# The gather of an expert's tokens, multiplied the other way round

## The reference

```python
def moe_ffn(h, router, w_gate, w_up, w_down):
    xt = h.reshape(B * S, D)
    logits = (xt @ router).astype(jnp.float32)
    top_v, top_i = lax.top_k(logits, TOP_K)              # TOP_K = 2
    top_w = jax.nn.softmax(top_v, axis=-1)
    gates = jnp.sum(jax.nn.one_hot(top_i, N_EXPERTS) * top_w[..., None], axis=1)
    out = jnp.zeros((B * S, D), jnp.float32)
    for e in range(N_EXPERTS):                           # N_EXPERTS = 8
        out = out + gates[:, e:e + 1] * swiglu(xt, w_gate[e], w_up[e], w_down[e])
    return out
```

## Time and profile before

| what | value |
|---|---|
| runs | 1356.06 us median of 3 (1355.68 to 1357.75) |
| profiled execution, span from the first to the last instruction | 1358.3 us; no other time is given for it |
| PE busy | 1297.8 us, 96% |
| DVE busy | 1046.4 us, 77% |
| ACT busy | 814.9 us, 60% |
| mean granted clock of TensorE | 0.973 of full speed |
| read from memory | 348.60 MB, 257 GB/s over the span |

### The profile page before, as it was taken

How to read it: one execution, slowest core, us unless ns; L and a number is a source line. 1 busy time by engine, 2 the same in 40 slices (tenths; PEclk the granted TensorE clock), 3 DMA queues, 4 the chain that set the end, 5 groups by cost and what they waited for, 6 DMA issues and landing times.

```text
span 1358.3 us, 17178 instructions
## 1 busy us (share of the span) xinstructions
PE 1297.8 (96%) x6105; PEld 1063.5 (78%) x6111; DVE 1046.4 (77%) x1014; ACT 814.9 (60%) x847; POOL 31.9 (2%) x29
## 2 busy tenths in 40 slices
PE   6999999999989997899999999999999999999997
PEld 5877878888778766688888888788887888888885
DVE  4786664444477945788998989889989889989986
ACT  5434354444335434577767767777776777777773
POOL 0130000000011000000000000000000000000000
PEclk9989999999989978799999999999999999999999
DMA  9540045554524302399999999999999899989992
GB/s 386 216 152 5 1 158 187 187 187 186 189 100 166 129 32 93 140 364 346 368 349 339 366 355 341 342 344 347 358 341 361 332 338 362 350 344 365 343 373 89
DMA packets 48635, 350.75 MB, mean 258 GB/s; under 512 B 5392, under 2 KB 5392, under 8 KB 6320
## 3 DMA queue, kind: packets, MB, share of 16 engines
q1 hardware_dynamic: 48560, 349.67, 68.5%
HBM read 348.60 MB, written 1.05 MB: 257 GB/s over the span
## 4 chain that ended last, share of the span: by engine, by line
PE 90%; DVE 5%; ACT 2%; issue 1%; POOL 1%; DMA 0%; SPq 0%; POOLq 0%; DVEq 0%; ACTq 0%
PE bank L490 26%; PE bank L492 26%; PE bank L491 26%; PE bank L922 1%; PE bank L652 1%; PE bank L798 1%; PE bank L678 1%; DVE wlo L1280 1%; ACT whi L1012 1%; PE bank L660 1%; PE bank L873 1%; PE bank L874 1%; PE bank L810 1%; PE bank L813 1%; PE bank L896 1%
## 5 line engine op out<-in xcount | busy, mean ns | idle before, releaser
L1854 DVE TENSOR_TENSOR wlo<-raw,whi 128x2048 fp32r<-128x2048 f32 x261 | 597.5, 2290 | 85.3 <-ACT whi L1207 82.2
L1207 ACT CAST whi<-raw 128x2048 fp32r<-128x2048 f32 x261 | 498.9, 1912 | 142.7 <-PE bank L492 142.3
L490 PE MATMUL bank<-whi,hT_hi 128*128 128x512 f32 (+1 forms) x1104 | 432.4, 392 | 9.2 <-DVE wlo L1280 3.9
L492 PE MATMUL bank<-whi,hT_lo 128*128 128x512 f32 (+1 forms) x1104 | 430.6, 390 | 2.7 <-issue 2.7
L491 PE MATMUL bank<-wlo,hT_hi 128*128 128x512 f32 (+1 forms) x1104 | 430.2, 390 | 0.0
L490 PEld LDWEIGHTS bank<-whi,hT_hi 128*128 128x128 f32 x1104 | 208.7, 189 | 55.1 <-issue 8.0
L1280 DVE TENSOR_TENSOR wlo<-raw,whi 128x2048 fp32r<-128x2048 f32 x68 | 155.7, 2291 | 122.3 <-ACT whi L1012 121.2
L492 PEld LDWEIGHTS bank<-whi,hT_lo 128*128 128x128 f32 x1104 | 208.5, 189 | 46.9 <-issue 3.6
L491 PEld LDWEIGHTS bank<-wlo,hT_hi 128*128 128x128 f32 x1104 | 208.6, 189 | 43.4 <-issue 0.2
L1012 ACT CAST whi<-raw 128x2048 fp32r<-128x2048 f32 x68 | 129.5, 1905 | 135.6 <-PE bank L492 135.4
L490 PE MATMUL bank<-whi,h_hi 128*128 128x512 f32 x440 | 181.6, 413 | 3.0 <-DVE h_lo L1543 3.0
(11 more groups left out here) (289 smaller groups left out, 979.1 us busy)
## 6 DMA issues: line engine op xcount, KB each, us to landing
raw<-in_weights SPq DMA_DIRECT2D x329, 1024.0 KB, 4.8
arena<-in_compress SPq DMA_DIRECT2D x1, 1088.0 KB, 14.6
x<-in_x SPq DMA_DIRECT2D x1, 1024.0 KB, 5.1
out<-x SPq DMA_DIRECT2D x2, 512.0 KB, 4.1
cst<-in_constants SPq DMA_DIRECT2D x1, 668.0 KB, 6.3
sml<-in_small SPq DMA_DIRECT2D x1, 402.0 KB, 6.8
msk_bits<-in_masks SPq DMA_DIRECT2D x1, 288.0 KB, 15.0
wa<-in_w_a SPq DMA_DIRECT2D x1, 64.0 KB, 15.0
```

Of the source, the lines that this page charges most:

```text
L490: mm(out_, a_hi, b_hi, start=start, stop=False)
L492: return mm(out_, a_lo, b_hi, start=False, stop=stop)
L1207: nc.scalar.copy(whi[:, u % SPLIT, :, :], raw[:, u % RAW, :, :]).then_inc(S["w_hi"], 1)
L1854: V.tensor_tensor(wlo[:, u % SPLIT, :, :], raw[:, u % RAW, :, :], whi[:, u % SPLIT, :, :].bitcast(F32), ALU.subtract).then_inc(S["w_lo"], 1)
```

## The change

`gather_rows` is gone. `gather` now multiplies with the tokens stationary and the dispatch matrix moving, so that features by slots come out at once: for each of the four 128-column blocks of a half it sums two token tiles and two parts in a 128x128 corner of bank 6 or 7, which makes 16 matmuls of 128 moving columns for a half. The two ACT copies, the transposes and their two semaphore waits are gone, DVE's multiplication reads bank 6 or 7 in place of bank 3, and the two halves stand in chunks 6 and 7 of PE's order, where the rows stood in chunk 6 and the transposes in 7 and 8. DVE's and ACT's steps behind it keep their places.

```diff
-            def gather_rows(e):
+            def gather(e, half):
 
                 pe.wait_ge(S["disp"], e + 2)
-                for half in range(2):
-                    c = slice(half * BLK, (half + 1) * BLK)
+                for j in range(4):
+                    k = half * 4 + j
+                    to = bank[6 + half][:, j * P:(j + 1) * P]
                     for t in range(NT):
-                        mm(bank[6 + half][:, :], disp[:, t, :], hn_hi[:, t, c], start=(t == 0), stop=False)
-                        last = mm(bank[6 + half][:, :], disp[:, t, :], hn_lo[:, t, c], start=False, stop=(t == NT - 1))
-                    last.then_inc(S["rows_psum"], 1)
-
-            def gather(e, half):
-
-                pe.wait_ge(S["rows"], (e + 1) * 2 + (half + 1))
-
-                if half or not isinstance(e, int) or e >= 0:
-                    pe.wait_ge(S["xg_tmp"], (e + 1) * 2 + half)
-                for j in range(4):
-                    c = slice((half * 4 + j) * P, (half * 4 + j + 1) * P)
-                    last = nc.tensor.transpose(bank[3][:, j * P:(j + 1) * P], hn[:, 0, c], ident)
+                        mm(to, hn_hi[:, t, k * P:(k + 1) * P], disp[:, t, :], start=(t == 0), stop=False)
+                        last = mm(to, hn_lo[:, t, k * P:(k + 1) * P], disp[:, t, :], start=False, stop=(t == NT - 1))
                 last.then_inc(S["xg_psum"], 1)
...
-                    if not drain and c == GATHER:
-                        gather_rows(e)
-                    if not drain and c in (GATHER + 1, GATHER + 2):
-                        gather(e, c - GATHER - 1)
+                    if not drain and c in (GATHER, GATHER + 1):
+                        gather(e, c - GATHER)
...
-            gather_rows(-1)
             gather(-1, 0)
             gather(-1, 1)
...
-            def gathered_rows(e):
-                for half in range(2):
-                    act.wait_ge(S["rows_psum"], (e + 1) * 2 + (half + 1))
-                    nc.scalar.copy(hn[:, 0, half * BLK:(half + 1) * BLK], bank[6 + half][:, :]).then_inc(S["rows"], 1)
...
-                    if not drain and c == GATHER:
-                        gathered_rows(e)
...
-                                bank[3][:, :].rearrange("p (k n) -> p k n", k=4),
+                                bank[6 + half][:, :].rearrange("p (k n) -> p k n", k=4),
```

More of the change, by code:

```diff
@@ L334, in trunk @@
             gla_rstd mixed first_rows logitsT_psum logitsT logits gap gap_exp picked rank route disp
-            combT_psum combT rows_psum rows xg_psum xg cur m_silu m_hact m_h2T_psum m_h2T ysb scat out""".split()
+            combT_psum combT xg_psum xg cur m_silu m_hact m_h2T_psum m_h2T ysb scat out""".split()
         S = {n: sem(n) for n in NAMES}
@@ L939, in expert @@
                 if second:
-                    gather_rows(e - 1)
                     gather(e - 1, 0)
@@ L1213, in expert @@
                 if second:
-                    gathered_rows(e - 1)
                     gathered(e - 1, par, 0)
@@ L1242, in expert @@
                     final_sums(e, (e + 1) * EXP_UNITS + U_MOE)
-            gathered_rows(-1)
             gathered(-1, 0, 0)
```

## The result

The changed kernel took 1364.64 us in the median of five runs (1363.55 to 1365.22), the kernel before 1357.75 on the same chip (1355.68 to 1360.19). The ratio is 1.0041 with a 95% interval of 1.0024 to 1.0058, which makes some 5.6 us more; the two medians lie 6.9 us apart. The forecast was +4.6 us, a median of 1360.7 and a range of 1357 to 1365: 1364.64 lies just inside its upper end. The sum came near, but not all its terms did.

A forecast was written before the change was run, and what follows sets the result against it. PE, busy for 96%, was taken as the bound. Gathers inside experts +6.9 us and the opening -2.3 summed to +4.6: 1358.3 becomes 1362.9, the median 1360.7, range 1357 to 1365.

The forecast's parts named there:

- PE is the only path: Expert stage: each microsecond in PE's stream moves the end; time taken off ACT or DVE, 1.17 us of copies per gather, nothing.
- A pair at 0.116 us, bounded by its load: Gathers inside experts: 32 pairs take 3.71 us, replacing 2.73; net +0.98 us per gather, seven times, +6.9 us.
- Rival (d): Gather pairs: narrow fp32r products take several passes, 0.215 us each; +29 us and opening +6, near 1391; chance 0.05.
- (b): Gather pairs: moving columns set the pace, loads hide; 0.064 us a pair, faster, 1349 us; chance 0.06.
- (c): Gather pairs: part of the load hides; 0.086 us a pair, nothing per gather, opening alone -2.3, 1353.8 us; chance 0.05.
- The opening: Gather before expert 0 and first products behind it: +0.5 - 0.9 - 1.9 = -2.3 us, ends +0.5 and -3.2.
- The +0.5 us for the gather itself: Gather before expert 0 at a clock of 0.5: expert's first product at 556.9 us where it stood at 556.33.
- I expect the rise within this stretch: Gather before expert 0: PE works unbroken for 6.8 us from 547.59, so the clock rises between 551.4 and 554.4.
- rival (a): Opening: the clock doesn't come back earlier; +6.9 + 0.5 = +7.4 us, 1363.5; chance 0.17.
- The -2.8 us of clock gain: Opening: an earlier clock rise takes 0.9 us off the gather and 1.9 us off the expert's first products.
- 2.7 us of waits for nothing: PE in the expert stage: it waits 2.7 us, twice, for no engine at all; no change was forecast.
- the -0.2 that the forecast's upper end takes for the opening: Upper end of the forecast's span: +7.8 from gathers inside experts, -0.2 from the opening, +7.6 us.

The follow-up runs named there:

- the last run: 12 fp32 products, 8 columns wide, added ahead of the loop in the changed kernel; ratio 1.0037 to the kernel before.
- the one before it: 12 fp32 products, 8 columns wide, added ahead of the loop in the kernel before; ratio 0.9968 to the kernel before.
- bf16 padding: 16 tiny bf16 products added behind the rows in every expert of the kernel before; 1374.5 us, ratio 1.0108.
- the 20 fillers: 20 fp32 products of 512 columns, which nobody reads, added in PE's opening gaps of the changed kernel; 1362.3 us, ratio 1.0028 to the kernel before.
- the fp32 padding: 16 tiny fp32 products added behind the rows in every expert of the kernel before; ratio 1.0053.

## Why the prediction was right, and where it was not

- *PE is the only path.* Right: 99.35 - 98.48 = 0.87 us per expert for pairs that cost 0.84; half the pairs brought 1.79 back; ACT's copies put back cost nothing (99.35).
- *A pair at 0.116 us, bounded by its load.* Right in kind, a little high: 0.1115 measured, and half the columns left it at 0.112. The term was +6.9 us and is 7 x 0.87 = +6.1. One bound was misread: the row of L829 (0.111) is one pass of a two-pass product. So are the rows of single columns, two products in four records, and of fp32 at 256 columns (0.215 a pass, 0.43 a product). Rival (d)'s "even a fall to plain fp32 costs nothing" was therefore wrong: 32 products in fp32 would have cost 0.22 us each. As a bound for one load the 0.111 held all the same. Rivals (b) and (c) would have needed pairs below 0.09 us; no fp32r pair here came under 0.109. The Trainium skill, "TensorE: Matmul & The Clock Gate", section "Back-to-back issue gap", gives about 81 ns for a pair with 128 moving columns; for fp32r the runs do not agree with it, and they decide.
- *The opening.* The +0.5 us for the gather itself is what came, of which the clock, rising 0.4 us sooner behind the first product, gave 0.2 back. The step that failed is "I expect the rise within this stretch": 7.06 us of narrow fp32r pairs without a break did not raise the clock, so rival (a) held for this term. The -2.8 us of clock gain did not come. Its size was right: with the clock held up by fillers the gather took 1.3 us less and expert 0 up to its single-column records 1.65 less (34.08 against 35.73). Wrong was what would bring the rise about. The expert's first product came at 557.82 and a clock of 0.5, not near 556 and 1.0. Two small slips stand in the ends: 0.5 - 1.7 - 1.9 is -3.1, not -3.2, and the -0.2 that the forecast's upper end takes for the opening has no working; neither moves the range by more than 1 us.
- *What was not in the sum.* The stops at the loop's jumps, which I saw as 2.7 us of waits for nothing and left as they were, fell by 3.9 us in the profiles. This is what kept the total near the forecast: the seven distances +2.1, the opening +0.3, and +4.3 with the 1.0 us from ahead of 529 us and the 0.9 in the tail. The runs say +4.7 to +5.6. Pairs and opening alone are +6.4 (6.1 + 0.3), nearer to rival (a)'s +7.4 than to the forecast's +4.6. One term that did not come and one that was not in the sum nearly cancelled: the mechanism of the pairs was foreseen, the closeness of the total was luck. With the placement shifted the same way in both kernels, in the last run against the one before it, the ratios differ by 0.0069, some 9 us give or take 4, of which 3.0 are stops (4.7 against 1.75), now on the changed kernel's side; some 6 remain for pairs and opening.

What stays open: why 12 products ahead of a loop change by up to 2 us what PE loses at each of its jumps, and why the loss ran from 0.4 to 9 us. The traces point to the fetching of instructions. Queue q8 (kind "instruction") moves a packet of 16 KB every 20 to 30 us. The six longest waits of PE around the jumps in the kernel before, in the one with half the pairs and in the one with bf16 padding, 1.0 to 5.8 us each, all ended 1.3 to 1.5 us after such a packet had landed; in the last of these, for one, it landed at 852.63 and PE went on at 853.98. In the changed kernel with the shift, two packets landed nearly together and PE went on 2.2 to 2.5 us later. The number of packets alone does not tell: with the 20 fillers and with the fp32 padding there are three around a jump, as before the change, at stops of 0.6 to 0.9 us. No run changed the fetching by itself, so the cause is argued and not shown.

## What to carry to other kernels

Turning a product round so that its narrow side moves makes the stationary load the price: count loads, not moving columns, before swapping operands on an engine that is the bound. Compare two kernels by the distance between repeated instructions inside the loop, and look at the loop's jumps apart, since a shift of the code moves them by as much as a change of this size. Where PE idles in a serial stretch, fillers that fit its gaps can be worth more than a faster step, but count passes when sizing them.

## What the runs showed of the hardware

- An fp32r pair with 128 stationary columns takes 0.11 us with 128 moving columns and with 64; an fp32 product is two passes with a load each, 0.224 us at 128 columns. An fp32 pass with 16 stationary columns and one moving column takes 0.025 us, one with 128 stationary columns 0.113.
- Seven us of narrow fp32r pairs without a gap left the granted clock at 0.5; in narrow fp32 passes at the same pace it rose after 3.3 us, at the same point of the kernel.
- PE's stops at a loop's backward jump ran from 0.4 to 9.0 us over loops that differ in little or nothing but the code around them; 12 products ahead of the loop moved them by 1.4 to 1.7 us down in one kernel and by 1.8 to 2.1 up in the other.
- Six of PE's waits around the jumps ended 1.3 to 1.5 us after a 16 KB packet of the instruction queue had landed.
